# A two-layer model on one core: the pieces of a norm alternate with the weight splits of the next chunk

## The chip, the cores and the metric

The kernel runs on one core of a Trainium2 chip. The metric is the device time in microseconds of one execution. The engines are named as in the profile: PE is the matmul engine (PEld its weight loads), DVE the vector engine, ACT the scalar engine, POOL the general one, SP the engine that here only issues DMAs. Each engine works through its own list of instructions in the order of the program; they meet at semaphores.

## The reference, cut to what matters

`reference` runs two blocks over x of 256 tokens by 2048. The first block has two layers (differential attention, then an S5 state space mixer, each followed by an MLP) and ends with a norm. The second block, the "second mixer" of the code, begins with a norm of its own and multiplies the result with a wide matrix `w_in`. The place of the change is the passage between the two:

```python
def first_block(x, ...):
    for i in range(DEPTH):
        ...
        x = x + mix
        x = x + sqrelu_mlp(rmsnorm(x, norm_mlp[i]), mlp_w1[i], mlp_w2[i])
    return rmsnorm(x, norm_final)

def _hybrid_layer(x, norm_gain, w_in, ...):
    h = _rmsnorm(x, norm_gain)
    u = h @ w_in
    ...
    return x + m @ w_out
```

So x is normed by `norm_final`, that result is kept as the residual, and it is normed again by `norm_gain` to feed `w_in` (2048 by 8392). Everything is fp32.

## The kernel before, in words

**Matmuls in split precision.** Each weight matrix is walked in chunks of 512 columns. A chunk has 8 units (`UNITS`) of 256 rows by 512 columns. For each unit, SP loads the fp32 weights into `raw` (4 buffers, `RAW`), ACT casts them to `wH` (L1688, 4 buffers, `SPLIT`), DVE subtracts and leaves the rest in `wL` (L2350, 4 buffers), and PE multiplies 12 times with 512 columns: eight matmuls with `wH` (the high and the low part of x, two halves of the tokens, two rows of blocks; L953 and L954), then four with `wL` and the high part of x (L960). A cast waits for its raw weights and for PE to be done with the unit four before it. A load waits for the subtraction four before it. `split(c, half, units=...)` on ACT and on DVE does this for units of chunk c.

**Order of the work.** `steps(n, evac, turned, ...)` (ACT L1690, DVE L2353) runs over n chunks. At step k an engine splits units 4 to 7 of chunk c0+k, does what is to be done with transposes of the chunk before, splits units 0 to 3 of chunk c0+k+1, and then evicts chunk c0+k. With `entered=True` the units 4 to 7 of the first chunk have been split before.

**The norm that runs behind its product.** The product of the first chunk with `w_in` (c0 in what follows) doesn't wait for a norm: x times both gains (`gain2`) is transposed and multiplied without the reciprocal roots, and the eviction (`second_out`, L2141 and on) scales each row with `rboth`, the product of both. Meanwhile DVE and ACT do the norms. `lead_ends` splits units 4 to 7 of c0 and takes the root of the first norm (`lead_rstd` on DVE, `lead_root` on ACT). Then DVE makes X the normed residual in eight pieces (L2924: four column quarters q, two halves m of the tokens, each releasing `x2_done`), ACT squares each quarter (`lead_square(q)`, L1790) once both its pieces are there, DVE sums (L2437), ACT takes the second root (`lead_root`, L1795), DVE inverts and multiplies (L2439, L2929). After the root ACT issues three small DMAs with constants (`mixmu`, `lmu`, `fbias`, L2104 to L2106), and DVE waits for all three (`f_in`, 48), writes one row of zeros (L2984) and enters `steps(9, ...)`. ACT enters its `steps(9, second_out, ...)` right after the DMAs. PE needs units 0 to 3 of c0+1 at once when c0 is done. In the middle of c0+1 it transposes the evicted c0 (`stg_turn`, L968).

Of the kernel before, what the change touches and what calls it, by code (L numbers as in the profile page):

```python
# [231 lines left out]
def build(nc, I, out):  # L232
    with ExitStack() as ctx:
        def sb(name, shape, dt=F32):
            return ctx.enter_context(nc.sbuf_tensor(name, shape, dt))
# [172 lines left out]
        small = sb("small", [P, 256])  # L408
# [1267 lines left out]
        def _(act):  # L1676
            t = Tally()

            def split(c, half, small=False, units=None):

                for j in units or range(half * HALF, half * HALF + HALF):

                    loads = j // RAW + 1
                    act.wait_ge(raw_in[j % RAW], c * (16 * UNITS // RAW) + (16 * loads * (2 if small else 1) + t.extra))

                    act.wait_ge(unit_used, c * UNITS + (j + 1))
                    n = LC if small else NW
                    nc.scalar.copy(wH[:, j % SPLIT, :, 0:n], raw[:, j % RAW, :, 0:n]).then_inc(high_done, 1)  # L1688

            def steps(n, evac, turned=None, small=None, entered=False):  # L1690

                c0 = t.chunk
                for k in range(n):
                    if k or not entered:
                        split(c0 + k, 1, k == small)
                    if k == small:
                        t.extra = 16 * UNITS // RAW
                    if turned is not None and k:
                        turned(k - 1)
                    split(c0 + k + 1, 0, k + 1 == small)  # L1700
                    evac(k)
                t.chunk += n

# [77 lines left out]
            def lead_square(q, count=1):  # L1781

                if q == QT - 1:

                    nc.scalar.activation(small[:, 103 + t.norm:104 + t.norm], eps, ACT.Sqrt)
                if q:

                    act.wait_ge(sumsq_done, MT * (QT * (t.norm - 1) + q))
                for m in range(MT):
                    nc.scalar.activation(wk[m][:].rearrange("p a s -> p (a s)"), X[:, m, q * NW:(q + 1) * NW], ACT.Square,  # L1790
                                         accum_out=ssq[:, m, q:q + 1]).then_inc(sumsq_done, 1)

            def lead_root():
                act.wait_ge(ssum_done, t.norm)
                nc.scalar.activation(std, ss, ACT.Sqrt, bias=eps, scale=1.0 / D).then_inc(std_done, 1)  # L1795
# [156 lines left out]
            c0 = t.chunk  # L1952
# [118 lines left out]
            c0, f0 = t.chunk, t.fill  # L2071
# [10 lines left out]
            def gate(c):  # L2082
# [6 lines left out]
                for m in range(MT):  # L2089
                    bank = acc[0][m][:] if c else tp[m][:].rearrange("p a s -> p (a s)")  # L2090
                    nc.scalar.activation(stg[:, (c // 2) % 2, m], bank, ACT.Sigmoid).then_inc(acc_free, 1)

            steps(8, gate, turned=glu_lead, entered=True)
            t.fill += 8
            t.x_ready = 4 + 2 * t.fill
# [4 lines left out]
            for q in range(QT):  # L2100
                act.wait_ge(x2_done, MT * (q + 1))
                lead_square(q)
            lead_root()
            act.dma_start(mixmu[:], I["rwkv_shift_mix_2"][:, 0:NW].broadcast_to([P, NW])).then_inc(f_in, 16)  # L2104
            act.dma_start(lmu[:], I["rwkv_shift_mix_2"][:, 4 * H1:].broadcast_to([P, 2 * LORA])).then_inc(f_in, 16)
            act.dma_start(fbias[:], I["fox_forget_bias_2"].broadcast_to([P, F_HEADS])).then_inc(f_in, 16)  # L2106
            c0, f0, g0 = t.chunk, t.fill, t.group
# [33 lines left out]
            def second_out(c):  # L2141
# [26 lines left out]
                if c > 16:  # L2168
                    n = c - 17
                    act.wait_ge(acc_free, 2 * (f0 + 16 + n) + 6)  # L2170
                    act.dma_start(gates[n // 4][:, :, (n % 4) * NW:(n % 4 + 1) * NW], stg[:, c % 2]).then_inc(gate_out[c % 2], 16)

            steps(9, second_out, turned=second_turned, small=4, entered=True)
            t.group += 8

            def fox_exp(i):
# [137 lines left out]
            def mixed_high(c):  # L2314
                for g in range(2):
                    high(g0 + 2 * c + g, None, g, hH[:, 4 * c + 2 * g:4 * c + 2 * g + 2])

            steps(4, lambda c: load_gates(c + 1) if c < 3 else None, turned=mixed_high, entered=True)
            t.fill += 8
            c0 = t.chunk  # L2320
# [21 lines left out]
        def _(dve):  # L2342
            t = Tally()

            def split(c, half, small=False, units=None):

                for j in units or range(half * HALF, half * HALF + HALF):
                    dve.wait_ge(high_done, c * UNITS + (j + 1))
                    n = LC if small else NW
                    nc.vector.tensor_tensor(wL[:, j % SPLIT, :, 0:n], raw[:, j % RAW, :, 0:n],  # L2350
                                            wH[:, j % SPLIT, :, 0:n].bitcast(F32), ALU.subtract).then_inc(split_done, 1)

            def steps(n, evac, turned=None, small=None, entered=False):  # L2353
                c0 = t.chunk
                for k in range(n):
                    if k or not entered:
                        split(c0 + k, 1, k == small)
                    if k == small:
                        t.extra = 16 * UNITS // RAW
                    if turned is not None and k:  # L2360
                        turned(k - 1)
                    split(c0 + k + 1, 0, k + 1 == small)
                    evac(k)
                t.chunk += n

# [270 lines left out]
            c0 = t.chunk  # L2636
# [15 lines left out]
            n = [0]  # L2652
# [234 lines left out]
            c0, f0 = t.chunk, t.fill  # L2887
# [5 lines left out]
            def glu(c):  # L2893
# [11 lines left out]
                lead_gain(c // 2, glu=MT * (c // 2))  # L2905

            steps(8, glu, turned=glu_lead, entered=True)
            t.fill += 8

# [10 lines left out]
            for q in range(QT):  # L2920
                cols = slice(q * NW, (q + 1) * NW)
                for m in range(MT):
                    x = X[:, m, cols]
                    nc.vector.scalar_tensor_tensor(x, x, rstd[:, m:m + 1], gain[:, cols], ALU.mult, ALU.mult).then_inc(x2_done, 1)  # L2924
            nc.vector.tensor_copy(rboth, rstd).then_inc(scale_own, 1)
            t.norm += 1
            lead_rstd()
# [2 lines left out]
            c0, f0 = t.chunk, t.fill  # L2930
# [51 lines left out]
                nc.vector.tensor_tensor(o, o, stg[:, c % 2], ALU.add).then_inc(shift_out, 2)  # L2982

            nc.vector.memset(prev[0:1, 0], 0.0).then_inc(shift_out, 1)  # L2984
            steps(9, lambda c: None, turned=second_turned, small=4, entered=True)
            t.fill += 24
            t.group += 8

# [288 lines left out]
            c0, f0, h0 = t.chunk, t.fill, t.high  # L3277
# [34 lines left out]
            c0 = t.chunk  # L3312
# [45 lines left out]
```

## Time and profile of the kernel before

| | us |
|---|---|
| median of 3 runs | 3050.01 (3048.55 to 3051.59) |
| the profiled execution, its own time | 3051.24 |
| its span in the trace | 3049.5 |
| PE busy | 2963.8 (97%) |
| PEld busy | 2465.2 (81%) |
| DVE busy | 1821.9 (60%) |
| ACT busy | 1379.8 (45%) |
| POOL busy | 343.0 (11%) |

Times in the trace count from the start of the span. PE is the engine that is nearly always busy, so the thing to look for is where it is idle or runs at a lower clock. Matmuls overlap by a part of their duration: one of 512 columns is listed with about 0.39 us, and they start 0.227 us apart at full clock. Ends of matmuls are modelled; starts are the better thing to read. Rows of several merged instructions give the start of the first and the time to the end of the last.

### The profile page before, as it was taken

The numbers are of one execution on the slowest core, as the hardware profiler recorded it, in microseconds if no ns is written. First come the engines' busy times: TensorE is split into PE (matmuls) and PEld (weight loads), VectorE is DVE, ScalarE is ACT, GpSimd is POOL, SyncE is SP. The second block draws the span as 40 slices with busy tenths as digits, with TensorE's granted clock in tenths as the row PEclk, the third lists the DMA queues.
The fourth block names the chain that finished last, engine by engine and source line by source line (L and its number), as shares of the span: only waits on it lengthen the run. The fifth ranks groups of instructions, "written<-read, shape, count | busy, mean of one in ns | idle before, by whom it ended". The sixth has DMA issues, their size and how long they took to land.

```text
span 3049.5 us, 45950 instructions
## 1 busy us (share of the span) xinstructions
PE 2963.8 (97%) x17927; PEld 2465.2 (81%) x17927; DVE 1821.9 (60%) x2046; ACT 1379.8 (45%) x1897; POOL 343.0 (11%) x367
## 2 busy tenths in 40 slices
PE   8999999999999997999999999999999999999898
PEld 6888788788888886888888888888788887878786
DVE  5555557955765667555555555556444667666764
ACT  5555444344443447444434444444544445550243
POOL 2000010950000766200000000000000000000000
PEclk9999999999999998999999999999999999999999
DMA  7555476675667886566666565665666667650364
GB/s 245 174 167 172 148 215 195 224 232 181 192 202 225 239 262 193 163 193 213 184 193 187 191 192 187 193 183 184 173 185 193 190 199 235 198 190 4 118 214 152
DMA packets 301956, 577.86 MB, mean 189 GB/s; under 512 B 21544, under 2 KB 40232, under 8 KB 300096
## 3 DMA queue, kind: packets, MB, share of 16 engines
q1 hardware_dynamic: 285696, 522.85, 55.9%
q0 software_dynamic: 10992, 43.07, 4.9%
q10 hardware_dynamic: 5072, 9.15, 1.0%
q8 instruction: 145, 2.38, 0.3%
q14 instruction: 51, 0.42, 0.0%
HBM read 547.22 MB, written 21.50 MB: 186 GB/s over the span
## 4 chain that ended last, share of the span: by engine, by line
PE 91%; DVE 5%; ACT 2%; DMA 1%; issue 1%; ACTq 0%; SPq 0%; DVEq 0%
PE acc L953 26%; PE acc L960 26%; PE acc L954 26%; DVE wL L2350 2%; PE tp L968 2%; PE acc L1660 1%; PE acc L1653 1%; PE acc L1654 1%; PE tp L1563 1%; PE acc L1561 1%; DMA raw<-in_mlp_w_dram 1%; ACT wH L1688 0%; PE acc L1254 0%; PE wk L1239 0%; ACT wk L1790 0%
## 5 line engine op out<-in xcount | busy, mean ns | idle before, releaser
L2350 DVE TENSOR_TENSOR wL<-raw,wH 128x1024 fp32r<-128x1024 f32 (+1 forms) x968 | 1225.8, 1276 | 1094.5 <-ACT wH L1688 1092.2
L1688 ACT CAST wH<-raw 128x1024 fp32r<-128x1024 f32 (+1 forms) x968 | 1009.2, 1046 | 1392.1 <-PE acc L960 1182.1
L953 PE MATMUL acc<-wH,xH 128*128 128x512 f32 (+1 forms) x2208 | 867.9, 394 | 6.6 <-DVE xL L2404 4.0
L954 PE MATMUL acc<-wH,xL 128*128 128x512 f32 (+1 forms) x2208 | 856.7, 389 | 0.0
L953 PE MATMUL acc<-wH,hH 128*128 128x512 f32 x1504 | 589.6, 392 | 1.9 <-DVE hL L2404 1.9
L960 PE MATMUL acc<-wL,xH 128*128 128x512 f32 (+1 forms) x2208 | 588.2, 388 | 1.2 <-DVE wL L2350 1.1
L954 PE MATMUL acc<-wH,hL 128*128 128x512 f32 x1504 | 586.3, 390 | 0.0
L953 PEld LDWEIGHTS acc<-wH,xH 128*128 128x128 f32 x2208 | 415.9, 188 | 95.3 <-issue 5.1
L960 PEld LDWEIGHTS acc<-wL,xH 128*128 128x128 f32 x2208 | 413.0, 188 | 87.5 <-DVE wL L2350 2.3
L954 PEld LDWEIGHTS acc<-wH,xL 128*128 128x128 f32 x2208 | 416.2, 188 | 82.9 <-issue 0.5
L960 PE MATMUL acc<-wL,hH 128*128 128x512 f32 x1504 | 404.4, 391 | 5.9 <-DVE wL L2350 5.7
L960 PEld LDWEIGHTS acc<-wL,hH 128*128 128x128 f32 x1504 | 282.0, 188 | 68.4 <-DVE wL L2350 10.2
L953 PEld LDWEIGHTS acc<-wH,hH 128*128 128x128 f32 x1504 | 283.3, 188 | 60.6 <-DVE hL L2404 2.4
L954 PEld LDWEIGHTS acc<-wH,hL 128*128 128x128 f32 x1504 | 283.3, 188 | 58.0
L881 POOL DMA_DIRECT2D prev<-stgs x8 | 4.3, 540 | 1097.8 <-ACT stgs L2167 1097.8
L2404 DVE TENSOR_TENSOR hL<-tp,hH 128x512 fp32r<-128x512 f32 x80 | 51.3, 683 | 6.2 <-ACT hH L1744 6.1
L1653 PE MATMUL acc<-wH,xH 128*128 128x512 f32 x128 | 51.4, 402 | 0.8 <-DVE xL L2404 0.6
L1654 PE MATMUL acc<-wH,xL 128*128 128x512 f32 x128 | 50.8, 397 | 0.0
L968 PEld LDWEIGHTS tp<-ident,stgs 128*128 128x128 f32 x384 | 45.0, 141 | 6.2
L968 PE MATMUL tp<-ident,stgs 128*128 128x128 f32 x384 | 49.7, 272 | 0.0
L1744 ACT CAST hH<-tp 128x512 fp32r<-128x512 f32 x80 | 42.8, 587 | 8.1 <-PE tp L968 8.1
L2454 DVE SCALAR_TENSOR_TENSOR X<-acc,small,X 128x512 f32<-128x512 f32 x64 | 44.9, 744 | 0.2
(492 smaller groups left out, 2160.3 us busy)
## 6 DMA issues: line engine op xcount, KB each, us to landing
raw<-in_mlp_w_dram SPq DMA_DIRECT2D x512, 512.0 KB, 3.8
raw<-in_w_in_dram SPq DMA_DIRECT2D x192, 512.0 KB, 4.0
raw<-in_a_w_in_dram SPq DMA_DIRECT2D x96, 512.0 KB, 3.7
raw<-in_b_w_glu_dram SPq DMA_DIRECT2D x64, 512.0 KB, 3.8
raw<-in_a_w_out_dram SPq DMA_DIRECT2D x32, 512.0 KB, 3.7
raw<-in_w_out_dram SPq DMA_DIRECT2D x32, 512.0 KB, 4.5
raw<-in_w_proj_fox_dram SPq DMA_DIRECT2D x16, 512.0 KB, 5.5
raw<-in_w_proj_rwkv_dram SPq DMA_DIRECT2D x16, 512.0 KB, 4.8
```

Of the source, the lines that this page charges most:

```text
L953: nc.tensor.matmul(bank, aH[:, k, rows], wH[:, j % SPLIT, u, 0:n], start=k == 0, stop=False)
L954: nc.tensor.matmul(bank, aL[:, k, rows], wH[:, j % SPLIT, u, 0:n], start=False, stop=False)
L960: last = nc.tensor.matmul(bank, aH[:, k, rows], wL[:, j % SPLIT, u, 0:n], start=False, stop=k == KT - 1)
L968: last = nc.tensor.transpose(dst, src, ident[:])
L1561: nc.tensor.matmul(B[2 + k][half[c], cols], XT[half[c], h], QQ[half[c], h], start=True, stop=True)
L1653: nc.tensor.matmul(bank, xH[:, k, rows], wH[:, j % SPLIT, u], start=k % 8 == 0, stop=False)
L1654: nc.tensor.matmul(bank, xL[:, k, rows], wH[:, j % SPLIT, u], start=False, stop=False)
L1688: nc.scalar.copy(wH[:, j % SPLIT, :, 0:n], raw[:, j % RAW, :, 0:n]).then_inc(high_done, 1)
L1744: nc.scalar.copy(dst, tp[bank][:]).then_inc(group_high, 1)
L2350: nc.vector.tensor_tensor(wL[:, j % SPLIT, :, 0:n], raw[:, j % RAW, :, 0:n], wH[:, j % SPLIT, :, 0:n].bitcast(F32), ALU.subtract).then_inc ...
L2404: nc.vector.tensor_tensor(dL, tp[bank][:], dH.bitcast(F32), ALU.subtract).then_inc(group_free, 1)
L2454: nc.vector.scalar_tensor_tensor(x, acc[par][m][:], rstd_sq[:, m:m + 1], x, ALU.mult, ALU.add).then_inc(acc_free, 1)
```

## The change

Only the order on ACT and DVE changes. Inside the loop over the four quarters of the norm, ACT splits unit q of the next chunk (`t.chunk + 1`) after the squares of quarter q, and DVE after the two pieces of quarter q. The first step of `steps` then skips those four units (`ahead=True`). No other engine's program changes.

```diff
@@ on ACT
-            def steps(n, evac, turned=None, small=None, entered=False):
+            def steps(n, evac, turned=None, small=None, entered=False, ahead=False):
 ...
-                    split(c0 + k + 1, 0, k + 1 == small)
+                    if k or not ahead:
+                        split(c0 + k + 1, 0, k + 1 == small)
                     evac(k)
                 t.chunk += n
@@ on ACT
             for q in range(QT):
                 act.wait_ge(x2_done, MT * (q + 1))
                 lead_square(q)
+                split(t.chunk + 1, 0, units=(q,))
             lead_root()
@@ on ACT
-            steps(9, second_out, turned=second_turned, small=4, entered=True)
+            steps(9, second_out, turned=second_turned, small=4, entered=True, ahead=True)
@@ on DVE
-            def steps(n, evac, turned=None, small=None, entered=False):
+            def steps(n, evac, turned=None, small=None, entered=False, ahead=False):
 ...
-                    split(c0 + k + 1, 0, k + 1 == small)
+                    if k or not ahead:
+                        split(c0 + k + 1, 0, k + 1 == small)
                     evac(k)
                 t.chunk += n
@@ on DVE
                 for m in range(MT):
                     x = X[:, m, cols]
                     nc.vector.scalar_tensor_tensor(x, x, rstd[:, m:m + 1], gain[:, cols], ALU.mult, ALU.mult).then_inc(x2_done, 1)
+                split(t.chunk + 1, 0, units=(q,))
             nc.vector.tensor_copy(rboth, rstd).then_inc(scale_own, 1)
@@ on DVE
-            steps(9, lambda c: None, turned=second_turned, small=4, entered=True)
+            steps(9, lambda c: None, turned=second_turned, small=4, entered=True, ahead=True)
```

## Rows read from the trace of the kernel before

**Rows 1.** The page, part 4: the chain that ended last, by engine.
```profile
PE 91%; DVE 5%; ACT 2%; DMA 1%; issue 1%; ACTq 0%; SPq 0%; DVEq 0%
```

**Rows 2.** Busy by stretch: length, PE, PEld, DVE, ACT, POOL, then PEclk, DMA, GB/s.
```profile
2140.00:2150.00 10.00, 9.84 (x44) 7.83 (x42) 7.39 (x15) 7.42 (x25) 0.00 (x0) 1.00 0.33 102
2150.00:2160.00 10.00, 6.83 (x18) 4.97 (x19) 5.09 (x6) 5.42 (x7) 0.00 (x0) 0.66 0.51 113
2160.00:2170.00 10.00, 10.00 (x50) 8.34 (x49) 4.91 (x4) 4.80 (x6) 0.00 (x0) 1.00 0.89 288
```

**Rows 3.** Waits of PE, 2130 to 2170 us: total, times, longest.
```profile
PE acc L953 <- ACT wH L1688: 2.2, 1, 2.2
PE acc L960 <- DVE wL L2350: 1.1, 1, 1.1
```

**Rows 4.** Timeline of PE: start, length, line, merged count, idle time before.
```profile
2146.06 1.07 PE L960 MATMUL acc<-wL,xH 128*128 128x512 f32 x4
...
2148.78 1.07 PE L960 MATMUL acc<-wL,xH 128*128 128x512 f32 x4
2152.04 0.47 PE L953 MATMUL acc<-wH,xH 128*128 128x512 f32 x1 [2.20 <-ACT wH L1688]
...
2156.01 2.08 PE L960 MATMUL acc<-wL,xH 128*128 128x512 f32 x4 [1.13 <-DVE wL L2350]
...
2160.67 1.09 PE L960 MATMUL acc<-wL,xH 128*128 128x512 f32 x4
...
2167.05 1.04 PE L968 MATMUL tp<-ident,stgs 128*128 128x128 f32 x8
2169.75 1.07 PE L960 MATMUL acc<-wL,xH 128*128 128x512 f32 x4
```

**Rows 5.** Timeline of DVE around the norm.
```profile
2142.20 5.39 DVE L2924 SCALAR_TENSOR_TENSOR X<-X,small,gains 128x512 f32<-128x512 f32 x8
...
2149.25 0.16 DVE L2437 TENSOR_REDUCE small<-small 128x2 f32<-128x8 f32 x1 [1.57 <-ACT wk L1790]
...
2154.39 0.48 DVE L2984 MEMSET prev<- 1x512 f32 x1 [4.26 <-DMA fbias<-in_fox_forget_bias_dram]
2154.81 4.55 DVE L2350 TENSOR_TENSOR wL<-raw,wH 128x1024 fp32r<-128x1024 f32 x4
2160.71 1.23 DVE L2350 TENSOR_TENSOR wL<-raw,wH 128x1024 fp32r<-128x1024 f32 x1 [1.35 <-ACT wH L1688]
```

**Rows 6.** Timeline of ACT around the norm.
```profile
2143.65 0.60 ACT L1790 ACTIVATE wk<-X 128x512 f32<-128x512 f32 x1 [1.68 <-DVE X L2924]
...
2144.80 0.19 ACT L1790 ACTIVATION_READ_ACCUMULATOR wk<-X 128x1 f32 x1
...
2147.66 0.19 ACT L1790 ACTIVATION_READ_ACCUMULATOR wk<-X 128x1 f32 x1
2147.75 0.19 ACT L1785 ACTIVATE small<-small 128x1 f32<-128x1 f32 x1
2147.88 0.60 ACT L1790 ACTIVATE wk<-X 128x512 f32<-128x512 f32 x1
...
2149.44 0.29 ACT L1795 ACTIVATE small<-small 128x2 f32<-128x2 f32 x1 [0.23 <-DVE small L2437]
...
2150.85 3.88 ACT L1688 CAST wH<-raw 128x1024 fp32r<-128x1024 f32 x4 [1.11 <-PE acc L960]
2154.64 1.25 ACT L2167 ACTIVATE stgs<-acc,small 128x512 f32<-128x512 f32 x2
2159.62 1.05 ACT L1688 CAST wH<-raw 128x1024 fp32r<-128x1024 f32 x1 [3.73 <-DMA raw<-in_w_in_dram]
```

**Rows 7.** SP's waits; DMA landings of raw weights, fbias, later mixmu (POOL).
```profile
SPq L520 <- DVE wL L2350: 32.1, 12, 14.0
...
DMA to landing us min/median/max: 3.5/4.4/5.4
...
DMA to landing us min/median/max: 3.9/3.9/3.9
...
DMA to landing us min/median/max: 6.5/6.8/7.6
```

## The prediction
> **What bounds the kernel now.** I read the page first. 91% of the chain that ended last is work of the matmul engine PE itself [rows 1], so a change can only pay where that engine stands still or is slow. The diff touches one place, so I went to that place with three views: the engine table by stretch, the waits of PE, and then the timelines of PE, DVE and ACT side by side.
>
> The place is the junction between the first chunk of `w_in_2` (call it c0) and the next one (c0+1). In 2150 to 2160 us PE is busy only 6.83 of 10 us and its granted clock averages 0.66; the stretches on either side are full and at 1.00 [rows 2]. PE waits twice, 2.2 us for ACT's cast into `wH` and 1.1 us for DVE's `wL` [rows 3]. The timeline gives the exact price. A unit (256 rows by 512 columns of weights, 12 matmuls) takes 2.72 us in steady state: 2146.06 to 2148.78 from one unit's last four matmuls to the next one's. c0 ends at 2148.78 + 0.91 = 2149.69 (the last four matmuls are 4 x 0.227). In steady state the two units behind it would have ended at 2149.69 + 5.44 = 2155.13. They end at 2160.67 + 0.93 = 2161.60 [rows 4]. **The stall costs 6.5 us**: 2.35 idle before unit 0 (from 2149.69 to 2152.04), 2.15 until its `wL` is there (8 matmuls at full clock would end at 2153.86, the `wL` ones start at 2156.01), and 2.0 because PE runs at the lower of its two levels (1.2 instead of 2.4 GHz) after the idle time.
>
> Why are the weights late? The norm stands in one block ahead of the splits on both engines. DVE does the eight pieces from 2142.20 to 2147.59, ACT follows with its squares, takes the root at 2149.44, issues three DMAs, and starts its four casts only at 2150.85 [rows 5, 6]. DVE, after the root, waits for the constants of those DMAs until 2154.39, writes one row, and starts the four `wL` at 2154.81 [rows 5].
>
> **The change, part by part.** No instruction is added or taken away. Four casts on ACT and four subtractions on DVE move from behind the root into the norm, one after each pair of pieces or squares. The wait that this adds is the point. ACT's cast q stands behind the squares q, which wait for DVE's pieces q. DVE's pieces q+1 stand behind the subtraction q, which waits for ACT's cast q. So the two engines take turns and never overlap. One turn, from rows:
> - pieces q to squares q: 2142.20 to 2143.65, 1.45 us;
> - squares to cast: the second read of the accumulator starts at 2144.80, and an instruction that waits for nothing starts 0.09 behind such a read (2147.66 to 2147.75), so 1.25 with rounding up;
> - cast to subtraction: 2159.62 to 2160.71, 1.09;
> - subtraction to the next pieces: four in 4.55 us, so (4.55 - 1.23)/3 = 1.11 apart; I take 1.13.
>
> The sum is 4.92 us for a turn [rows 5, 6]. PE uses a unit in 2.72. **The interleaved block makes units at little more than half the speed at which PE eats them**, and only its early start (2142.20 instead of 2150.85) gives a lead.
>
> Turn q starts at 2142.20 + 4.92q. The casts end at 2145.95, 2150.87, 2155.79 and, with the small extra root instruction of the last quarter (2147.75 to 2147.88, 0.13), 2160.84; the subtractions end at 2147.2, 2152.1, 2157.1 and 2162.1. The casts have their slots: cast q needs PE to be done with unit 4+q of c0, and going back from 2149.69 in steps of 2.72 those end at 2141.5, 2144.3, 2147.0 and 2149.7. The raw weights are there too: the queue of loads waits 14.0 us for a buffer until the first subtraction ends at 2156.04, so the last of them was issued by about 2142.1 and with the longest landing of the stretch, 5.4 us, is in by 2147.5 [rows 7].
>
> PE then goes like this. Unit 0: no wait, 2149.69 to 2152.41. Unit 1: no wait, to 2155.13; here the whole 6.5 us is gained. Unit 2: its cast ends at 2155.79, PE wakes 0.14 later, so it starts at 2155.93 (**wait 0.8**) and ends at 2158.65. Unit 3: cast at 2160.84, start 2160.98 (**wait 2.3**), end 2163.70.
>
> Behind unit 3 stands what the block pushed back. DVE's copy and sum follow its last subtraction, so the root R comes at about 2162.35 instead of 2149.44, **12.9 us later**. With it moves all that hangs on it, at the distances of before [rows 5, 6]:
> - the three DMAs that ACT issues right after R. What stands next on ACT starts at R + 1.41 (2149.44 to 2150.85); that is now the eviction of c0, two instructions in 1.25 us, from 2163.8 to 2165.0. PE's transposes at the middle of c0+1 need it (**wait 1.4**); eight take 0.9 (from 2167.05 to the start of unit 4, which is its end, 2170.66, less 2.72), so 2165.1 to 2166.0;
> - the cast of unit 4, which ends at 2166.0, so unit 4 starts at 2166.1 (0.1);
> - DVE's wait for the constants: R + 4.95, then the row, and the subtraction of unit 4 starts at R + 5.37 = 2167.7 and ends at 2168.95. PE has done eight matmuls of unit 4 by 2167.9 (**wait 1.1**) and ends unit 4 at 2169.9.
>
> Before, unit 4 ended at 2169.75 + 0.91 = 2170.66 [rows 4]. So the waits of 0.8 + 2.3 + 1.4 + 0.1 + 1.1 = 5.7 us take the place of 6.5: a gain of 0.8 us before two unknown terms.
>
> **First unknown, the constants.** Before, no weights moved when they were loaded (that same wait of 14.0 us), and `fbias` landed in 3.9 us. Now the load of unit 7 is released by the last subtraction at 2162.1, in the same microsecond. The cost is from 0 (landing 3.9 as before) to 3.7 us (7.6, the worst of the seven later `mixmu` loads, which do run beside weight loads but are issued by POOL) [rows 7]. Weight loads themselves land in 3.5 to 5.4 us here, a spread of 1.9; as one load alone is in flight beside the constants I take half of it less a little, 0.8 us.
>
> The Trainium skill ("DMA: Bandwidth & Descriptors", section on queues, rings and completion order) says that each DMA engine takes packets in turn from all queues that have work. By that the constants would be held up by no more than the packets of the one load; by a first-come order they would pass it altogether and the sum would be 0.8 us lower. No row of before shows the two together at this place.
>
> **Second unknown, the clock.** Before, PE's idle 2.35 us ahead of unit 0 was followed by the lower level, worth 2.0 us [rows 2, 4]. Now the longest idle time is 2.3 us, ahead of unit 3, so the same may happen. But the slack behind unit 3 is 1.4 + 0.1 + 1.1 = 2.6 us, in which PE waits anyway. A drop costing 2.0 us fits into it. Bounds: 0 to 2.0; a gain is excluded, since the sum already runs every matmul at the higher level. I take 0, by the slack.
>
> Nothing else moves time. Raw buffers come free earlier (2147 instead of 2156), so units 4 to 7 are in SBUF long before ACT gets to them, and the next chunk's first loads start at about 2169.7 and are needed at 2178. POOL has nothing in this stretch.
>
> **Sum.** -0.8 + 0.8 + 0 = 0.0 us. The profiled execution took 3051.24 (span 3049.5), the median of the runs shown is 3050.01, and the three lie 3.0 us apart. I forecast **3050.0**.
>
> **Rivals.**
> - Forecast, the stall is cut up and moved: 3049.2 to 3052.9 with the bounds of the first unknown (-0.8 to +2.9). Chance 0.80.
> - The stall really goes. For it, units 0 and 1 are ready early without doubt. Against it, the turns of 4.92 us against 2.72 follow from the program's order. If the turns took as little as 2.7 us (pieces and squares beside casts), all 6.5 us would go: 3043.5. Half of it, if squares and cast of a turn hid behind DVE's part: 3046.8. Chance 0.08, a third of it beyond 0.2%.
> - Slower by one mechanism: DVE's wait for the constants, which was hidden in part behind the stall, now holds `wL` of unit 4 while weights stream. At 7.6 us landing it costs 3.7 instead of 0.8, PE waits 4.8 us there, the clock falls behind that wait (2.0 more, no slack left to hide it), and the time is 3050.0 - 0.8 + 3.7 + 2.0 = 3054.9. It is slower than before as soon as the constants are more than 0.8 us late; it passes 0.2% when they are 4.9 us late with the clock, beyond any row. Chance 0.10, a third of it beyond 0.2%.
> - The change does nothing because the casts wait for PE's slots or for raw weights: the rows exclude it (slots free 2141.5 to 2149.7). 0.02.
>
> **How the numbers follow.** 0.2% is 6.1 us, about what a measurement of this kernel can tell from no change. The whole stall at stake is 6.5 us, so only a complete success could show: faster 0.03, slower 0.04, within 0.2% 0.93. The range takes the forecast's bounds, half of the gain rival and most of the slow one's reach, with the 3 us by which runs differ: 3046.5 to 3053.5.
>
> **What would show it.** In the profile after: PE without a wait between c0 and c0+1; waits for `wH` of 0.8 and 2.3 us ahead of units 2 and 3; pairs of pieces on DVE 4.9 us apart with idle time between; the root near 2162.4; a wait for `stg` and one for `wL` in unit 4; unit 4's last matmuls within 2 us of 2169.75. I am wrong if pieces stand closer than 4 us, if the root comes before 2158, or if PE's position at the end of unit 4 is off by more than 3 us.

## The result and the profile after

| | us |
|---|---|
| before, median of 18 runs | 3049.85 (3047.41 to 3053.74) |
| after, median of 18 runs | 3054.81 (3050.84 to 3058.74) |
| ratio of the times, after to before | 1.0014, 95% interval 1.0008 to 1.0020 |
| the profiled execution of after, its own time | 3050.88 |
| its span in the trace | 3049.2 |

The change makes the kernel slower by 0.08 to 0.20%, 2.4 to 6.1 us. The forecast was 3050.0 and no change. The median of after lies above the forecast's range (3046.5 to 3053.5), and the difference from before is clear of noise, though it stays within the 0.2% to which the prediction gave a chance of 0.93.

The profiled execution of after is one of its three shortest. It has to be read with that in mind: it shows what the change always does, and not all that it does in the median.

The chain that ended last, by engine, answering to [rows 1]:

```profile
PE 91%; DVE 5%; ACT 2%; issue 1%; DMA 0%; ACTq 0%; SPq 0%; DVEq 0%
```

It tells nothing of so small a change. The stretches of after, answering to [rows 2] (length, PE, PEld, DVE, ACT, POOL, PEclk, DMA, GB/s):

```profile
2150.00:2160.00 10.00, 8.50 (x37) 6.38 (x35) 5.10 (x6) 4.76 (x13) 0.00 (x0) 1.00 0.38 114
2160.00:2170.00 10.00, 6.07 (x28) 4.46 (x28) 2.93 (x7) 7.08 (x10) 0.00 (x0) 1.00 0.39 99
2170.00:2180.00 10.00, 9.62 (x42) 7.99 (x43) 6.56 (x7) 3.54 (x5) 0.00 (x0) 1.00 0.78 253
```

The hole moved: it was in 2150 to 2160, now 2160 to 2170 is the emptiest (6.07 busy), and the granted clock is 1.00 throughout. The waits of PE in after, from 2140 to 2185 us, answering to [rows 3] (total, times, longest):

```profile
PE acc L953 <- ACT wH L1688: 2.4, 2, 2.0
PE acc L960 <- DVE wL L2352: 2.2, 1, 2.2
PE tp L968 <- ACT stgs L2169: 1.2, 1, 1.2
```

Four waits stand where there were two. The timeline of PE in after (start, length, idle time before it in brackets), answering to [rows 4]:

```profile
2148.98 1.07 PE L960 MATMUL acc<-wL,xH 128*128 128x512 f32 x4
2151.70 1.07 PE L960 MATMUL acc<-wL,xH 128*128 128x512 f32 x4
2154.42 1.07 PE L960 MATMUL acc<-wL,xH 128*128 128x512 f32 x4
2155.96 0.50 PE L953 MATMUL acc<-wH,xH 128*128 128x512 f32 x1 [0.47 <-ACT wH L1688]
...
2160.94 0.50 PE L953 MATMUL acc<-wH,xH 128*128 128x512 f32 x1 [1.97 <-ACT wH L1688]
...
2165.12 1.09 PE L968 MATMUL tp<-ident,stgs 128*128 128x128 f32 x8 [1.17 <-ACT stgs L2169]
...
2170.38 1.20 PE L960 MATMUL acc<-wL,xH 128*128 128x512 f32 x4 [2.21 <-DVE wL L2352]
...
2178.67 1.07 PE L960 MATMUL acc<-wL,xH 128*128 128x512 f32 x4
```

Units 0 and 1 follow c0 without a pause, then units 2, 3, the transposes and `wL` of unit 4 are each waited for. DVE in after, answering to [rows 5]:

```profile
2142.40 1.42 DVE L2927 SCALAR_TENSOR_TENSOR X<-X,small,gains 128x512 f32<-128x512 f32 x2
2146.15 1.22 DVE L2352 TENSOR_TENSOR wL<-raw,wH 128x1024 fp32r<-128x1024 f32 x1 [2.34 <-ACT wH L1688]
2147.29 1.41 DVE L2927 SCALAR_TENSOR_TENSOR X<-X,small,gains 128x512 f32<-128x512 f32 x2
2151.05 1.23 DVE L2352 TENSOR_TENSOR wL<-raw,wH 128x1024 fp32r<-128x1024 f32 x1 [2.35 <-ACT wH L1688]
2152.19 1.41 DVE L2927 SCALAR_TENSOR_TENSOR X<-X,small,gains 128x512 f32<-128x512 f32 x2
...
2160.92 1.23 DVE L2352 TENSOR_TENSOR wL<-raw,wH 128x1024 fp32r<-128x1024 f32 x1 [2.43 <-ACT wH L1688]
...
2168.76 0.48 DVE L2988 MEMSET prev<- 1x512 f32 x1 [5.75 <-DMA fbias<-in_fox_forget_bias_dram]
```

The pairs of pieces stand 4.90 us apart, and in each turn DVE waits 2.3 to 2.4 us for the cast of its own turn. The root on ACT and the landing of the last constant, `fbias`, answering to [rows 6] and [rows 7]:

```profile
2162.32 0.30 ACT L1796 ACTIVATE small<-small 128x2 f32<-128x2 f32 x1 [1.43 <-DVE small L2440]
```
```profile
DMA to landing us min/median/max: 5.4/5.4/5.4
```

**A ruler for the place.** Whole times carry differences from elsewhere (below), so the place is measured by itself: from the first piece of the norm on DVE to the start of the last four matmuls of unit 7 of c0+1. In a kernel without any wait there (the block version, below) this is 29.24 us. What is over that is the cost of the place.

| execution | its time | first piece | unit 7 | distance | over 29.24 |
|---|---|---|---|---|---|
| before, the trace of the prediction | 3051.24 | 2142.20 | 2177.91 | 35.71 | 6.5 |
| before, second trace | 3049.59 | 2141.76 | 2175.42 | 33.66 | 4.4 |
| after | 3050.88 | 2142.40 | 2178.67 | 36.27 | 7.0 |
| after, beside the experiments | 3051.82 | 2143.31 | 2179.76 | 36.45 | 7.2 |
| after, extra trace 1 | 3053.97 | 2141.12 | 2181.10 | 39.98 | 10.7 |
| after, extra trace 2 | 3051.21 | 2139.51 | 2175.81 | 36.30 | 7.1 |
| after, extra trace 3 | 3054.93 | 2142.75 | 2182.43 | 39.68 | 10.4 |

Before costs 4.4 or 6.5, after 7.0 to 7.2 or 10.4 to 10.7. Between a trace of before and one of after the loss is thus anywhere from 0.6 us (36.27 less 35.71) to 6.3 (39.98 less 33.66); best against best it is 2.6. The mean of the five rows of after is about 3 us above that of the two of before (8.5 and 5.4). The other two parts of a trace don't tell the kernels apart: the first piece starts at 2139.5 to 2143.3 in after and at 2141.8 and 2142.2 in before, and from unit 7 to the end of the span it is 870.3 to 873.7 in after, 871.6 and 872.5 in before.

### The profile page after: what moved, and what is told of

Its sections match the earlier page's. It is cut to its first block, busy times and chain, and to the rows that moved or that the text cites. A ratio compares the mean times of both kernels' runs of the same rounds, so it can differ in the third digit from the quotient of the medians.

```text
span 3049.2 us, 45950 instructions
## 1 busy us (share of the span) xinstructions
PE 2962.7 (97%) x17927; PEld 2464.4 (81%) x17927; DVE 1825.5 (60%) x2046; ACT 1379.4 (45%) x1897; POOL 341.1 (11%) x367
## 4 chain that ended last, share of the span: by engine, by line
PE 91%; DVE 5%; ACT 2%; issue 1%; DMA 0%; ACTq 0%; SPq 0%; DVEq 0%
PE acc L953 27%; PE acc L960 26%; PE acc L954 26%; DVE wL L2352 2%; PE tp L968 2%; PE acc L1660 1%; PE acc L1653 1%; PE acc L1654 1%; PE tp L1563 1%; PE acc L1561 1%; ACT wH L1688 0%; PE wk L1239 0%; PE acc L1254 0%; PE acc L1255 0%; ACT dd L2029 0%
```

## The experiments

Theory A: turns of 4.9 us push the root back, the constants with it land late beside a weight load, and the lower clock follows PE's idle time in some executions. Rivals: the clock has no part (B); the turns alone are all of it and the constants don't matter (C); the norm in one block is what costs, as the change supposes (D).

**1. The changed kernel again**, beside the experiments.

> The changed kernel itself once more, beside the others, for a second trace and a second set of times. Theory A (turns, constants, clock): the casts come 4.9 us apart again, the constants make wL of unit 4 late, and the clock after the idle stretches differs from run to run; ratio 1.001 to 1.002, and the longer runs have the lower mean granted clock (0.988 against 0.991). Theory B (the waits alone, the clock has no part): the time sits 2 to 3 us above before with no relation to the mean clock.

Measured: 3056.95 us in the median of 11 (3051.82 to 3058.90), ratio 1.0016 (1.0007 to 1.0025). Of the 18 runs of the first table, the three with a mean granted clock of 0.991 lie between 3050.8 and 3053.3 us and the five with 0.988 between 3056.2 and 3058.7. A forecast that. But it can't tell A from B: the mean clock counts the whole kernel, and the 33 runs of the kernel before that were taken beside this one are split in the same way (all at 0.988 lie at 3053.6 or more, all at 0.991 or above under 3049.3). A and B are told apart by experiments 4 and 9.

**2. The constants ahead of the norm.**

```diff
             lead_ends(added)
             t.norm += 1
+            act.dma_start(mixmu[:], ...)   # likewise lmu, fbias
             for q in range(QT):
...
             lead_root()
-            act.dma_start(mixmu[:], ...)   # likewise lmu, fbias
-        lmu = at("gain", 5.75, "lmu", [P, 2 * LORA])
-        fbias = at("gain", 6.5, "fbias", [P, F_HEADS])
+        lmu = at("mix", 40, "lmu", [P, 2 * LORA])
+        fbias = at("mix", 41, "fbias", [P, F_HEADS])
```

(Two of the tiles shared memory with the gain that the pieces read.)

> The changed kernel with its three DMAs of constants issued ahead of the norm loop (two of the tiles stand elsewhere in SBUF for that). Takes away DVE's wait behind the root. Theory A: wL of unit 4 comes with its cast (about 2167.3 in place of 2170.4), the 2.2 us idle time of PE there goes, and with it most of the lower clock that follows in some runs: 3 to 5 us less than the changed kernel, so about the time of before (3048 to 3051), and a narrower spread. Theory B (clock has no part): 2.4 us less. Theory C (the constants don't matter, the excess is from the turns of 4.9 us alone): no change from the changed kernel.

Measured: 3047.61 us (3044.92 to 3049.51), ratio to before 0.9986 (0.9977 to 0.9995). That is 9.3 us under the changed kernel in the medians, where 3 to 5 were expected, and the spread is narrow. PE's waits in this kernel from 2140 to 2185 us:

```profile
PE acc L953 <- ACT wH L1688: 2.4, 2, 2.0
PE tp L968 <- ACT stgs L2169: 0.4, 1, 0.4
```

The wait for `wL` is gone, and the one for `stgs` is 0.7 shorter (0.43 and 1.17 in the timelines), since ACT no longer issues DMAs between the root and the eviction. The place costs 3.8 us over the ruler (2175.24 less 2142.18 is 33.06), 3.2 less than in the best execution of after and 6.9 less than in the worst. The 9.3 of the medians is more than that explains. C falls: the turns cost 3.8 with the constants out of the way, which is less than the place costs in either trace of before.

**3. DVE in one block, ACT interleaved.** The turns go, nothing else.

```diff
                 for m in range(MT):
                     ...scalar_tensor_tensor(x, x, rstd[:, m:m + 1], gain[:, cols], ...).then_inc(x2_done, 1)
-                split(t.chunk + 1, 0, units=(q,))
+            split(t.chunk + 1, 0)
```

> ACT as in the changed kernel (squares q, cast q), but DVE does its eight pieces in one block and then the four subtractions, ahead of the root. Takes away the turns and nothing else. Theory A: casts end near 2146, 2148.5, 2150.8 and 2153.3, the root comes near 2154.6, the constants near 2160, PE finds every unit ready, no idle time and no lower clock at the place: 4.5 to 6.5 us under before, about 3044 to 3045.5. Theory C' (the casts and squares of one engine are simply too much work for this place, in whatever order): no faster than before.

Measured: 3044.91 us (3042.07 to 3049.89), ratio to before 0.9978 (0.9969 to 0.9987). The profiled execution is its longest. It shows no wait of PE in the place. The stretch 2150 to 2160, and DVE:

```profile
2150.00:2160.00 10.00, 10.00 (x46) 8.29 (x45) 7.59 (x12) 7.66 (x18) 0.00 (x0) 1.00 0.50 152
```
```profile
2147.02 5.39 DVE L2927 SCALAR_TENSOR_TENSOR X<-X,small,gains 128x512 f32<-128x512 f32 x8
2152.32 2.35 DVE L2352 TENSOR_TENSOR wL<-raw,wH 128x1024 fp32r<-128x1024 f32 x2
2155.13 1.23 DVE L2352 TENSOR_TENSOR wL<-raw,wH 128x1024 fp32r<-128x1024 f32 x1 [0.46 <-ACT wH L1688]
...
2165.44 0.48 DVE L2988 MEMSET prev<- 1x512 f32 x1 [5.96 <-DMA fbias<-in_fox_forget_bias_dram]
```

C' falls: the same instructions on the same engines fit into the place and PE never waits. The work was not too much, its order was wrong. DVE still waits 5.96 us for the constants, longer than in after, and nobody feels it, because the root comes about 11.8 us behind the first piece (0.33 ahead of the inversion at 2159.13) and not 19.9.

**4. After, with PE's idle time filled.**

```diff
+                def warmed(at, j):
+                    k, bank = (warm or {}).get((at, j), (0, None))
+                    for _ in range(k):
+                        nc.tensor.matmul(bank..., xH[:, 0, 0:P], xH[:, 0:2]..., start=True, stop=True)
...
+    warm={("high", 2): (2, tp[0]), ("high", 3): (8, tp[0]), ("mid", 4): (5, tp[0]), ("low", 4): (9, wk[0])} if c == 1 else None
```

> The changed kernel with 24 more matmuls of 512 columns that only fill PE's four idle stretches of chunk c0+1 (2 ahead of unit 2, 8 ahead of unit 3, 5 ahead of the transposes, 9 ahead of wL of unit 4), into banks that nobody reads. The waits stay, the idle time goes. Theory A: the granted clock is 1.00 from 2150 to 2180 in the trace, the slow runs vanish, the time is that of the fastest runs of the changed kernel: 3050.5 to 3052, that is 2 to 4 us less in the median. Theory B (the clock has no part): the median stays at 1.0014 times before or rises by up to 1 us.

Measured: 3052.48 us (3049.42 to 3056.49), 4.5 under the changed kernel beside it in the medians, ratio to before 1.0001 (0.9992 to 1.0010). Granted clock and two of the fillings:

```profile
2160.00:2170.00 10.00, 9.80 (x46) 7.55 (x45) 1.86 (x6) 6.76 (x12) 0.00 (x0) 1.00 0.55 141
```
```profile
2160.48 1.98 PE L941 MATMUL tp<-xH 128*128 128x512 f32 x8
...
2169.68 2.20 PE L941 MATMUL wk<-xH 128*128 128x512 f32 x9
```

By the ruler the place costs 7.2 us (2180.54 less 2144.07 is 36.47), just as in the executions of after without the lower clock. So 24 useless matmuls lower the median, and what they change is that PE is not idle while it waits. The median was expected to gain 2 to 4 us and gained a little more; B gives no gain. By the times alone that is support and not proof: the intervals of the two ratios to before (1.0007 to 1.0025 without the filling, 0.9992 to 1.0010 with it) overlap a little, and the one trace with the clock at 1.00 is matched by two of the unfilled kernel. The longest runs did not vanish altogether (3056.49), so part of the spread is not from this place.

**5. Before, with the constants ahead of the norm** (the edit of experiment 2, on the kernel before).

> The kernel before with the three DMAs of constants issued ahead of the norm loop, nothing interleaved. Theory A (what holds PE is the path root, DMA issues, constants, row): ACT's casts start right behind the root (1.3 us earlier), so unit 0 waits about 1.1 us in place of 2.35, its wL needs no constants and comes in time, the clock stays up: 4 to 5.5 us less than before, 3045 to 3046.5. Theory D (the norm in one block is what costs, as the change supposes): 1 to 2 us less at most.

Measured: 3045.89 us (3041.93 to 3049.50), ratio 0.9984 (0.9975 to 0.9993). PE's only wait in the place:

```profile
PE acc L953 <- ACT wH L1688: 1.0, 1, 1.0
```

The ruler gives 1.2 us (2174.30 less 2143.84 is 30.46) where before costs 4.4 to 6.5. D falls: most of what before loses here has nothing to do with the norm's order. It is the DMA issues and the constants between the root and the splits.

**6. Before, with PE's idle time filled** (10 matmuls ahead of `wH` of unit 0, 8 ahead of its `wL`).

> The kernel before with 18 more matmuls that only fill PE's two idle stretches of unit 0 (10 ahead of wH, 8 ahead of wL). Theory A: the wait stays (4.5 us), the lower clock behind it goes: 1 to 2 us less in the median than before, and less gained than by the same filling of the changed kernel (4.5 us in the medians). Theory B: no gain, or 0.3 us more from filling past the end of the wait.

Measured: 3049.42 us (3048.15 to 3055.27), 2.0 under before in the medians, ratio 0.9995 (0.9986 to 1.0004), which doesn't exclude no change. The place costs 4.9 us in its trace (2176.18 less 2142.03 is 34.15) with the granted clock at 1.00, against 4.4 and 6.5 in the two traces of before. It points where A points, no more.

**7. The block and the early constants together** (edits of 3 and 2).

> DVE's pieces in one block with its subtractions behind them, ACT interleaved, and the constants issued ahead of the loop. The look at the block without this showed no wait of PE, so theory A says: the same as that kernel within 1 us (3044 to 3045.5), since a wait that holds nobody is worth nothing. If the constants had a cost of their own (their traffic beside the weights), 1 to 2 us less than it.

Measured: 3045.26 us (3042.43 to 3052.23), ratio 0.9983 (0.9974 to 0.9992); no wait of PE in the place, the same as experiment 3 within noise. A wait that holds nobody is worth nothing.

**8. ACT's half of the change alone.** (DVE's half alone can't be tried: its first subtraction would wait for a cast that stands behind squares which wait for DVE's last pieces.)

```diff
# DVE as in the kernel before: no split in the loop, and
-            steps(9, lambda c: None, turned=second_turned, small=4, entered=True, ahead=True)
+            steps(9, lambda c: None, turned=second_turned, small=4, entered=True)
```

> Only ACT's half of the change: squares and casts alternate on ACT, DVE keeps the order of before (pieces, root, constants, then the four subtractions). The casts are early, the root comes near 2153.5, the constants 5 to 6.5 us behind it, so the first subtraction ends near 2160 to 2161 and PE, which has wH of unit 0 at once, waits some 8.7 us for wL, at the lower clock behind that. Theory A: 3 to 6 us more than before, 3053 to 3056. If the order on DVE did not matter: faster than before.

Measured: 3052.79 us (3047.82 to 3057.16), 1.4 over before in the medians and ratio 1.0002 (0.9992 to 1.0012). That is no difference from before that could be told from noise, where 3 to 6 us more were expected. The trace has the wait:

```profile
2159.91 2.08 PE L960 MATMUL acc<-wL,xH 128*128 128x512 f32 x4 [6.91 <-DVE wL L2352]
```
```profile
2158.30 0.48 DVE L2987 MEMSET prev<- 1x512 f32 x1 [3.83 <-DMA fbias<-in_fox_forget_bias_dram]
```

The place costs 9.4 us in this execution (2182.16 less 2143.55 is 38.61), with the lower clock for part of it (0.89 and 0.77 in the stretches from 2150 and 2160); that execution took 3056.62. The wait is shorter than the 8.7 us expected, because the constants come sooner: no weight load stands beside them here, and `fbias` lands in 4.1 us, as in before and not as in after. The order of the events is as expected. The median is not, and I have no trace of a short run that would say why.

**9. Three more traces of after, one of before.**

> A look at one more execution of the changed kernel. The traces so far show only its shortest executions (3051 to 3052 us), with no lower clock at the place. Theory A: an execution of 3054 us or more shows a granted clock under 1.00 somewhere in 2160 to 2185 us, behind one of the idle stretches (1.9, 1.2 or 2.4 us), and is late by 1.5 to 4 us there. Theory B: the clock at the place is 1.00 in all of them, and the longer time comes from elsewhere.

> As for the look before: theory A has a lower clock at the place in every execution over 3054 us, theory B in none.

> A third look at the changed kernel: theory A has a lower clock at the place in every execution over 3054 us, theory B in none.

> A look at one more execution of the kernel before. Its trace on record has the clock at the lower level from 2153 to 2160 us, worth 2.0 us. Theory A: that too comes in some executions only; without it units 0 and 1 of the chunk take 4.5 us more than in steady state, not 6.5.

Extra trace 1 (3053.97 us): stretch 2170 to 2180, and PE from the transposes on.

```profile
2170.00:2180.00 10.00, 9.98 (x32) 7.96 (x33) 5.81 (x5) 2.55 (x3) 0.00 (x0) 0.70 0.80 260
```
```profile
2163.85 1.09 PE L968 MATMUL tp<-ident,stgs 128*128 128x128 f32 x8 [1.17 <-ACT stgs L2169]
2170.02 2.07 PE L960 MATMUL acc<-wL,xH 128*128 128x512 f32 x4 [3.12 <-DVE wL L2352]
2175.30 1.40 PE L960 MATMUL acc<-wL,xH 128*128 128x512 f32 x4
2178.38 1.07 PE L960 MATMUL acc<-wL,xH 128*128 128x512 f32 x4
```

PE waits 3.12 us for `wL` and then runs at the lower level: unit 4's last four matmuls take 2.07 instead of 1.07, and the next unit's start 5.28 us later instead of the 2.85 of after. Extra trace 3 (3054.93 us) is the same with a wait of 2.74:

```profile
2171.26 2.08 PE L960 MATMUL acc<-wL,xH 128*128 128x512 f32 x4 [2.74 <-DVE wL L2352]
```

Extra trace 2 (3051.21 us) has the lower clock too, but ahead of that wait:

```profile
2160.00:2170.00 10.00, 7.97 (x33) 5.94 (x32) 4.22 (x6) 6.11 (x8) 0.00 (x0) 0.85 0.49 119
```
```profile
2158.05 0.50 PE L953 MATMUL acc<-wH,xH 128*128 128x512 f32 x1 [1.96 <-ACT wH L1688]
...
2160.44 1.91 PE L960 MATMUL acc<-wL,xH 128*128 128x512 f32 x4
2162.24 1.40 PE L968 MATMUL tp<-ident,stgs 128*128 128x128 f32 x8
2167.52 1.20 PE L960 MATMUL acc<-wL,xH 128*128 128x512 f32 x4 [2.02 <-DVE wL L2352]
```

Here unit 3 is slow, the wait for `stgs` vanishes into it, and the place costs 7.1 us, nothing more than without a drop. So in these traces **the lower clock is free when it falls into unit 3 and dear when it falls behind the last wait**. The second trace of before shows the same on the other side:

```profile
2150.00:2160.00 10.00, 8.33 (x28) 6.25 (x29) 4.96 (x5) 5.84 (x7) 0.00 (x0) 0.83 0.45 133
```
```profile
2151.60 0.66 PE L953 MATMUL acc<-wH,xH 128*128 128x512 f32 x1 [2.19 <-ACT wH L1688]
...
2155.32 1.21 PE L960 MATMUL acc<-wL,xH 128*128 128x512 f32 x4
```

Here the lower clock comes earlier and for a shorter time (0.83 in the stretch, not 0.66). It covers the eight matmuls with `wH` of unit 0, which have to wait for `wL` anyway, and the level is back for the four with `wL` (1.21 us, not 2.08). The place costs 4.4 us and not 6.5. B falls for the executions with the dear drop: behind the wait for `wL` of unit 4, extra traces 1 and 3 need 2.8 and 2.9 us more for the same matmuls than after does.

## Why the prediction was wrong

The turns and the root came out as forecast. What failed are two terms of the sum, the clock taken as 0 in after and the 6.5 us taken as the cost of the place before; a third, the constants, was sized too low.

- **Turns of 4.92 us that pace PE**: right, 4.90. The waits ahead of units 2 and 3 (forecast 0.8 and 2.3) end at 2155.96 and 2160.94, where 2155.93 and 2160.98 were forecast. (The trace of after stands 0.2 us later as a whole, so each is 0.2 earlier than forecast.) Counted from the starts of the matmuls, as the prediction did, the waits are 0.6 and 2.1; the listed idle times are shorter, 0.47 and 1.97, as they go by modelled ends. All in all the place costs 7.0 us in this trace, where the sum had 5.7 + 0.8 = 6.5 for after.
- **The root 12.9 us later**: right, 2162.32 for 2162.35. The transposes start at 2165.12 for 2165.1.
- **The constants, 0.8 us late**: this term was mis-sized. `fbias` lands in 5.4 to 6.3 us in the five traces of after, against 3.9 and 3.7 in before, and DVE's row starts 6.4 to 7.4 us behind the root instead of 4.95: 1.5 to 2.4 us late. The one weight load that I named is issued in the same moment as the first constant (2162.3 in after) and takes 5.9 to 6.4 us in the five, where the load one turn earlier, which stands alone, takes 3.5 to 3.8. Where no weight load stands beside the constants, in both traces of before and in experiments 6 and 8, `fbias` lands in 3.7 to 4.2. That load and constants are both late agrees with the rule of the Trainium skill ("DMA: Bandwidth & Descriptors", section on queues, rings and completion order) that a DMA engine takes packets in turn from its queues. My error in size was to halve the spread of other loads. The sentence on a first-come order was wrong in itself: by my own sum the load is released at 2162.1, ahead of the root at 2162.35, so by such an order the constants would stand behind the load and not pass it. The matmuls with `wL` of unit 4 start at 2170.38, where the sum had 2169.0 + 0.8.
- **The clock, 0 us**: this step failed. I saw slack behind unit 3 and let it pay for a drop there; extra trace 2 shows that this much is right. But I did not ask what follows the last of the new waits. Behind `wL` of unit 4 there is no slack. The wait there is 2.0 to 3.1 us long by the listed idle times, where the sum had 1.1 + 0.8, and in two of five traces the clock falls at it. Those two cost 3.7 us (extra trace 1) and 3.4 us (extra trace 3) more than after in the table; 0.9 and 0.5 of it are the still later constant (`wL` of unit 4 starts 28.90 and 28.51 us behind the first piece, not 27.98), the other 2.8 and 2.9 the clock.
- **The base of the sum**: this failed quietly. I set the waits of after against 6.5 us, the cost of the place in the one execution that I had, with 2.0 of lower clock in it, and took 0 for the clock in after. The other trace of before costs 4.4. A sum that has the clock on one side only compares a bad execution of before with a good one of after. Like for like, without its share on either side, it would have been 5.7 + 0.8 against 4.5: 2.0 us slower.
- **The rival on the slow side** was this mechanism: constants late, `wL` of unit 4 held, the clock behind it, 3054.9 us. It got a chance of 0.10. What came is 3054.81, with the constants 1.5 to 2.4 us late and not 3.7, the clock worth 2.8 and only in some executions, and the base too high. That the two numbers meet within 0.1 us is luck.
- **The signs of being wrong** did not fire: the pieces stand 4.90 us apart, the root comes at 2162.32, and the last matmuls of unit 4 start at 2170.38. No sign was set for what comes behind unit 4, and the dear drop is there. Also, unit 7's weights were not there long before ACT got to them: its cast waits 0.3 us for them in after. PE doesn't feel that.

What stays open: the table accounts for 0.6 to 2.8 us between before and the executions of after without the dear drop, and for 4.0 to 6.3 with it; the medians differ by 5.0 (by the interval 2.4 to 6.1). How often each case occurs is not known from five traces. The longest of them took 3054.93 us, and half of the runs of after took longer than that, so nothing here shows what the executions of 3055 to 3059 us look like. Experiments 2 and 3 are 9.3 and 12.0 us under the changed kernel beside them in the medians, while the place explains 3.2 to 6.9 and 7.0 to 10.7.

## What to carry to other kernels

When two engines are interleaved, write down who waits for whom within a turn: if each waits for the other, the turn is the sum of both engines' work, and it has to be no longer than the time that the consumer takes for what one turn makes (here 4.90 us against 2.72). In this case it was better to interleave the engine that feeds and leave the other in a block: 0.2% faster than before, the lowest median of all that ran, with the kernel before plus early constants (experiment 5) within the same interval. Issue small loads of constants long before the instruction that waits for them, and never sum one execution's waits with the clock against another's without it.

## What the runs showed of the hardware that I had not expected

The same program with nearly the same waits has the lower clock at this place in some executions and not in others: the changed kernel has none after 2.21 and 2.39 us of idle time, has it after 2.74 and 3.12 (0.66 and 0.70 of full in 2170 to 2180), and in one execution already after 1.96 (extra trace 2). The kernel before has it in both traces, after 2.20 and 2.19 us, for a shorter time in the second. With matmuls that compute nothing in the gaps, the median of after was 4.5 us lower and its one trace had 1.00 throughout the place.

The place is not where the remaining spread comes from. Its first piece starts anywhere from 2139.51 to 2147.02 us in these kernels, whose programs are the same up to there, and the block version spreads from 3042.1 to 3049.9 with no wait in the place. In 1140 to 1200 us the granted clock differs from trace to trace, and the first piece goes with it: 0.77 in four traces with the first piece at 2139.5 to 2142.2, 0.74 in seven with 2141.1 to 2143.8, 0.72 in two with 2144.1 and 2147.0, and 0.66 in one with 2146.4 (experiment 7). That this earlier stage makes the difference is likely by these numbers, and it was not tried. Behind unit 7 of c0+1 the rest of the kernel takes 870.2 to 873.7 us in these traces, which is a further part of the spread.
